# Projections with the norm's root behind the product, reordered column chunks, and head-norm products on GpSimd

## The reference

```
x32 * rsqrt(mean(x32 * x32) + eps) * gain       # norm
z = h @ w_in                                    # first block: 2208 columns
z = xn @ w_in                                   # second block: 3212 columns
```

## Time and profile before

| | |
|---|---|
| median of 3 runs | 2364.22 us (2364.0 to 2368.03) |
| profiled execution | 2368.23 us, of which the span of the trace is 2366.4 us |
| busy | PE 88%, DVE 73%, PEld 56%, ACT 35%, POOL 28% |
| granted TensorE clock, mean | 0.956 |

### The profile page before, as it was taken

How to read it: one execution, slowest core, us unless ns; L and a number is a source line. 1 busy time by engine, 2 the same in 40 slices (tenths; PEclk the granted TensorE clock), 3 DMA queues, 4 the chain that set the end, 5 groups by cost and what they waited for, 6 DMA issues and landing times. The chain is left out here.

```text
span 2366.4 us, 27745 instructions
## 1 busy us (share of the span) xinstructions
PE 2077.3 (88%) x8634; PEld 1325.0 (56%) x8634; DVE 1718.5 (73%) x4157; ACT 832.0 (35%) x2042; POOL 672.2 (28%) x625
## 2 busy tenths in 40 slices
PE   7999999999979999998777788798999997777886
PEld 6779987679979665544222333396655542233332
DVE  6757777677767477778787777574776777787875
ACT  6656655666657521111111111275311211111110
POOL 1300001200001033444444444110243444444541
PEclk9999999999989899999999999998899999999999
DMA  6245432335545369999999999754499999999996
GB/s 221 107 180 181 185 137 81 138 125 186 186 141 160 132 244 420 420 421 421 421 421 422 421 420 421 270 157 152 178 420 420 421 421 421 421 422 421 421 421 264
DMA packets 138668, 700.51 MB, mean 296 GB/s; under 512 B 14392, under 2 KB 40248, under 8 KB 66872
## 3 DMA queue, kind: packets, MB, share of 16 engines
q0 software_dynamic: 73728, 536.90, 54.7%
q1 hardware_dynamic: 64824, 162.22, 19.6%
HBM read 698.03 MB, written 1.05 MB: 295 GB/s over the span
## 5 line engine op out<-in xcount | busy, mean ns | idle before, releaser
L2045 PE MATMUL bank<-ARENA 128*128 128x512 f32 x2048 | 993.7, 632 | 207.0 <-DVE ARENA L2345 205.9
L2045 PEld LDWEIGHTS bank<-ARENA 128*128 128x128 f32 x2048 | 387.8, 199 | 792.0 <-DVE ARENA L2345 415.6
L2335 DVE CUSTOM_DVE_ANT_0 ARENA<-ARENA 128x1024 f32<-128x1024 f32 x512 | 626.1, 1223 | 258.8 <-DMA ARENA<-in_uv_rows,ARENA 251.4
L1941 POOL DMA_INDIRECT ARENA<-in_uv_rows,ARENA x512 | 573.9, 1121 | 762.5 <-PE bank L2045 644.2
L154 PE MATMUL bank<-PARTS,PARTS 128*128 128x256 f32 (+3 forms) x1424 | 460.7, 324 | 12.3 <-DVE PARTS L284 7.1
L155 PE MATMUL bank<-PARTS,PARTS 128*128 128x256 f32 (+6 forms) x1488 | 470.6, 316 | 0.0
L156 PE MATMUL bank<-PARTS,PARTS 128*128 128x256 f32 (+6 forms) x1488 | 470.0, 316 | 0.0
L2153 ACT ACTIVATE ARENA<-ARENA 128x1 f32<-128x1 f32 x512 | 103.9, 203 | 1028.3 <-DVE ARENA L2335 1027.4
L155 PEld LDWEIGHTS bank<-PARTS,PARTS 128*128 128x128 f32 (+2 forms) x1488 | 285.4, 192 | 13.6 <-issue 1.0
L156 PEld LDWEIGHTS bank<-PARTS,PARTS 128*128 128x128 f32 (+2 forms) x1488 | 285.0, 192 | 13.8
L154 PEld LDWEIGHTS bank<-PARTS,PARTS 128*128 128x128 f32 x1424 | 273.4, 192 | 33.0 <-DVE PARTS L284 7.8
(11 more groups left out here) (265 smaller groups left out, 1934.3 us busy)
## 6 DMA issues: line engine op xcount, KB each, us to landing
ARENA<-in_w_up_tiles SPq DMA_DIRECT2D x44, 1024.0 KB, 7.0
ARENA<-in_w_down SPq DMA_DIRECT2D x44, 512.0 KB, 3.3
ARENA<-in_w_out SPq DMA_DIRECT2D x32, 512.0 KB, 4.2
ARENA<-in_wq_tiles SPq DMA_DIRECT2D x16, 1024.0 KB, 11.6
ARENA<-in_w_in SPq DMA_DIRECT2D x40, 384.0 KB, 4.0
ARENA<-in_w_in SPq DMA_DIRECT2D x24, 512.0 KB, 9.0
ARENA<-in_w_in SPq DMA_DIRECT2D x40, 256.0 KB, 2.9
ARENA<-in_uv_rows,ARENA POOLq DMA_INDIRECT x512, 23.0
```

The source lines that it names most:

```text
L1941: nc.gpsimd.indirect_dma_start(out=slot[i % SLOTS], out_offset=None, in_=table[:, :], in_offset=bass.IndirectOffsetOnAxis(ap=picked[:, t, ...
L2045: last = mm(row_banks[t][n][:, :], diag[i % N_DIAG], slot[i % SLOTS][:, D + n * 512:D + (n + 1) * 512], start=(c == 0), stop=(c == NPICK - ...
L2335: v.tensor_tensor_reduce(u, u, xn[:, t, :], 1.0, 0.0, ALU.mult, ALU.add, dots[:, t, c:c + 1]).then_inc(S("dots_ready"), 1)
```

## The change

The norm's root moves behind the product in four places (both first-block layers and both second-block layers). TensorE transposes X itself; the gain is still multiplied in before the product, and each row of z is multiplied by the root when ScalarE takes it out of PSUM (`mul` in place of `copy`). For a turned chunk the root is a factor of the columns: VectorE builds two diagonal tiles, TensorE multiplies them by a matrix of ones, VectorE copies the result (rstd_cols), and VectorE takes the chunk out of PSUM by a product with it (`qk_scaled`); ScalarE's fourth tap then reads that copy. In the second block the transposes go column by column, and the squares are taken after the first eight weight units.

The first weights of the second block's first layer are loaded during the first block's last feed-forward net. The chunks are reordered, so that the third chunk is followed by the gate chunk and the output gate (2304) comes between the convolved ones. Much of the interleaved work is put behind other units. The products of the head norms go from VectorE to GpSimd. Of the zero products of the first block 18 of 32 stay.

```diff
+            def pe_by_columns(pe):
+                for k in range(KD):
+                    for t in range(NT):
+                        last = nc.tensor.transpose(bank[(k + first) % 8][:, t * P:(t + 1) * P],
+                                                   X[:, t, k * P:(k + 1) * P], ident)
+                    last.then_inc(S(tag + "_turned"), 1)
...
+        IN_COLUMNS = [(0, 384), (384, 384), (1152, 256), (2688, 268), (2304, 384), (1408, 256), (2956, 256), (1664, 256),
+                      (768, 384), (1920, 384)]
...
-                            last = nc.scalar.copy(z[:, t, n0:n0 + w], in_bank(c, t)[:, 0:w])
+                            last = nc.scalar.mul(z[:, t, n0:n0 + w], in_bank(c, t)[:, 0:w], STAT[:, 120 + t:121 + t])
...
+                    else:
+                        load_w_in_2(sp, 0, 0, PIECES)
...
-                        keep_busy(32)
+                        keep_busy(18)
...
-            in_chunks = [("rows", 0, 384, z[:, :, 0:384]), ("rows", 384, 384, z[:, :, 384:768]), ("turned", 1152, 256, 0),
-                         ("rows", 2688, 268, z[:, :, ML_IF:ML_IF + 268]), ("turned", 1408, 256, 2),
-                         ("rows", 2956, 256, z[:, :, SG_UV + 256:SG_UV + 512]), ("turned", 1664, 256, 4),
-                         ("rows", 2304, 384, og), ("rows", 768, 384, sbv), ("rows", 1920, 384, vaug[:, :, :, 0:HD])]
+            in_to = [("rows", z[:, :, 0:384]), ("rows", z[:, :, 384:768]), ("turned", 0),
+                     ("rows", z[:, :, ML_IF:ML_IF + 268]), ("rows", og), ("turned", 2),
+                     ("rows", z[:, :, SG_UV + 256:SG_UV + 512]), ("turned", 4),
+                     ("rows", sbv), ("rows", vaug[:, :, :, 0:HD])]
...
+                        act.wait_ge(S("qk_scaled"), d0 // 2 + 1)
                         for i in range(2):
                             f = d0 + i
-                            nc.scalar.copy(qkc[:, f, :], out_bank(c, i)[:, 0:T])
-                            last = nc.scalar.activation(qkm[:, f, :], out_bank(c, i)[:, 0:T], ACT.Identity,
+                            last = nc.scalar.activation(qkm[:, f, :], qkc[:, f, :], ACT.Identity,
                                                         scale=conv[:, f, 3:4], bias=conv[:, f, 4:5])
...
+                def qk_scaled(dve, c):
+                    d0 = in_chunks[c][3]
+                    dve.wait_ge(S("in2_used"), KD * (c + 1))
+                    for i in range(2):
+                        last = nc.vector.tensor_tensor(qkc[:, d0 + i, :], out_bank(c, i)[:, 0:T], rstd_cols, ALU.mult)
+                    last.then_inc(S("qk_scaled"), 1)
```

ScalarE's stream of the second block:

```diff
-                        if k == 7:
+                        if k == 7 and in_chunks[c - 1][0] == "rows":
                             act_take(act, c - 1)
+                        if k == 0 and c >= 2 and in_chunks[c - 2][0] == "turned":
+                            act_take(act, c - 2)
...
-                        if (c, k) == (7, 1):
+                        if (c, k) == (8, 1):
+                            attend.magnitudes(act, 0, 1)
+                            act.wait_ge(S("m_ready"), 1)
+                            nc.scalar.activation(row(6), row(6), ACT.Exp, scale=-1.0).then_inc(S("em_ready"), 1)
+                        if (c, k) == (8, 3):
+                            attend.logs(act, 0, 1)
+                        if (c, k) == (8, 4):
                             act.drain()
                             nc.scalar.activation(uv, z[:, :, SG_UV:SG_UV + 512], ACT.Gelu_apprx_tanh)
                             act.drain()
                             nc.scalar.activation(vsq_f, uvf, ACT.Square).then_inc(S("sgv_squares"), 1)
-                        if (c, k) == (8, 0):
-                            attend.magnitudes(act, 0, 1)
-                        if (c, k) == (8, 2):
-                            attend.logs(act, 0, 1)
...
```

VectorE's stream:

```diff
-                        if c in (4, 6, 8) and k < 3:
-                            last = tap(c - 2, k)
+                        if k == 7 and in_chunks[c - 1][0] == "turned":
+                            qk_scaled(dve, c - 1)
...
+                        if c in (4, 7, 9) and 1 <= k < 4:
+                            last = tap(c - 2, k - 1)
...
-                        if (c, k) == (4, 5):
-                            dve.wait_ge(S("sb_rstd"), 1)
-                            tt(sq12, sbqk, view(ss12, (12, NT), (1, 12), (0, HD)), ALU.mult)
-                        if (c, k) == (4, 7):
-                            dve.drain()
-                            tt(sqf, sqf, view(sbg, (0, NT), (1, 768)), ALU.mult).then_inc(S("sb_ready"), 1)
...
-                        if (c, k) == (7, 6):
+                        if (c, k) == (8, 0):
                             attend.scaled(dve, 0)
                             attend.scaled(dve, 1)
-                        if (c, k) == (8, 4):
+                        if (c, k) == (8, 5):
                             attend.softplus(dve, 0)
                             attend.softplus(dve, 1)
```

GpSimd's stream and TensorE's:

```diff
+                    pool.drain()
+                    nc.gpsimd.tensor_tensor(sq12, sbqk, view(ss12, (12, NT), (1, 12), (0, HD)), ALU.mult)
+                    pool.drain()
                     pool.wait_ge(S("mix2_params"), N_PARAMS)
+                    nc.gpsimd.tensor_tensor(sqf, sqf, view(sbg, (0, NT), (1, 768)), ALU.mult).then_inc(S("sb_ready"), 1)
                     nc.gpsimd.tensor_tensor(sgw, sgw, const("tril_t", (0, SGG), (1, P)), ALU.mult).then_inc(S("sgw_ready"), 1)
...
+                    nc.gpsimd.tensor_tensor(uvv, uvv, view(ss4, (4, NT), (1, 4), (0, HD)), ALU.mult)
+                    pool.drain()
+                    nc.gpsimd.tensor_tensor(uvf, uvf, view(svg, (0, NT), (1, SGG * HD)), ALU.mult).then_inc(S("uv_ready"), 1)
...
+                        if (c, k) == (1, 7):
+                            pe.wait_ge(S("rstd_diag"), 1)
+                            nc.tensor.matmul(bank[7][:, 0:T], const("ones"), view(rstd_diag, (1, T)),
+                                             start=True, stop=True).then_inc(S("rstd_spread"), 1)
-                        if (c, k) == (4, 6):
+                        if (c, k) == (4, 4):
                             turn_if()
-                        if (c, k) == (5, 1):
+                        if (c, k) == (5, 0):
                             turn_sb()
...
-                        if (c, k) == (8, 2):
+                        if (c, k) == (8, 1):
                             attend.suffix_sums(pe, 0)
                             attend.suffix_sums(pe, 1)
```

193 lines of the change are left out of this document (97 added, 96 removed).

## The result

The changed kernel is slower, by half a per cent. Its median is 2377.6 us (5 runs, 2375.63 to 2378.18), that of the kernel before 2368.03 (5 runs, 2364.0 to 2368.88); the measured ratio is 1.0049 with an interval of 1.0037 to 1.0061, which is 11.6 us (the two medians stand 9.6 us apart). Run again beside the experiments it gave 1.0067 (1.0047 to 1.0086). 2376 was forecast.

The account below looks back on a forecast made before the run. TensorE was taken to bound the second block's projection. Its layers' +7.6 and +8.0 with the first block's -2.1 and -1.6 gave +11.9 us, 2380.1 against the profiled execution, carried to the median as 2376; range 2357 to 2386.

Parts of the forecast that it names:

- The starts: Layers' first products come earlier: -2.1 and -1.6 us in the first block, -5.1 and -6.3 in the second.
- GpSimd: Fifth chunk, second block: GpSimd's head products hold VectorE's two-input instructions, so TensorE waits; +7.7 us in each layer.
- Rival A: Fifth chunk: VectorE is not held by GpSimd's long products; 2 x 7.7 us go, 2361; chance 0.18.
- The suffix sums: TensorE waits 8.0 us for softplus behind ScalarE's gelu, plus 1.7 for a half clock: +9.7 in each layer.
- Rival B: The suffix wait is short, as VectorE and ScalarE run ahead in chunk 7; 2357; chance 0.08.
- The scores: Second block: TensorE's wait for sb_low ahead of the scores grows by 0.5 us in each layer.
- The clock: Second block's half clocks: +1.7 us behind each long wait, -1.7 at each start, -2.9 behind layer 1's scores.
- rival C: Neither long wait, at GpSimd's products or the suffix sums, comes and all small gains hold; 2341; chance 0.08.
- D: The half clock lasts 12 us once in each layer: +8.6 us, 2385; chance 0.10.

Follow-up runs that it names:

- f9: The changed kernel run once more, unaltered; ratio to the kernel before 1.0067 (1.0047 to 1.0086).
- e1: The changed kernel with only the two head-norm products put back on VectorE; ratio to the kernel before 1.0029.
- e6: The kernel before with only the two head-norm products put on GpSimd; one run, 2381.8 us.
- e5: The changed kernel with each of GpSimd's two head-norm products cut into six instructions of 256 elements; ratio to the kernel before 1.0022.
- e4: The changed kernel with head-norm products on VectorE, and ScalarE's gelu and TensorE's suffix sums both moved behind unit (8, 5); ratio to the kernel before 1.0021.
- e7: The kernel before with the root behind the product and new starts, old chunk order, head and gate products on VectorE; ratio to the kernel before 1.0014.
- f11: e4 with 15 products of zeros on TensorE ahead of the first scores; ratio to the kernel before 1.0014.
- g12: The kernel before with zero products in TensorE's waits: 13 ahead of the second block's transposes, 11 ahead of the scores; ratio to the kernel before 1.0011.
- e8: The changed kernel with zero products in TensorE's two long waits, 16 behind unit (4, 2) and 30 behind (8, 1); ratio to the kernel before 1.0035.
- e2: The changed kernel with only ScalarE's gelu and its squares moved behind unit (8, 5); ratio to the kernel before 1.0044.

## Why the prediction was right

**The starts.** The forecast said -5.1 and -6.3 in the second block. From the engines' leaving the barrier (689.08, 1531.07) to the first product it takes 3.3 and 3.1 us, where it took 8.65 and 8.67: -5.3 and -5.6. The -6.3 took the transposes at full clock, 0.14 us each; they ran at 0.21, in a half clock, so the product is 3.1 us behind the barrier and not 2.4. In the first block -2.1 was forecast. The product starts 0.3 us earlier there (13.01 for 13.28), and the squares of the next layer 0.6 earlier (348.92 for 349.54): -0.6. The step that failed is the product's time of 12.2: the four high halves start at 10.10, not at 9.6, and the product waits for a weight's low half that VectorE makes behind four of the norm's. In the second layer -1.6 was forecast; the product comes at 351.39 for 354.54, 3.15 earlier, of which 2.5 are its own. At the barrier only 1.1 of these 3.1 us were left. In this profile a half clock near 490 us lasts 7 us where it lasted 3; it differs between the runs (7 in f9 too). The half clock behind the second block's starts was to go: it cost 1.7 us at each before, and costs 1.3 and 0.3.

**GpSimd.** +7.7 in each layer was the forecast, of it 6.0 idle. The waits were 0.57 and 4.11, 4.7 us; the forecast was too high. GpSimd's first product began at 721.89, before the chunk, as the whole stretch lay earlier; and the products took 3.0 and 3.6 us, not 3.8 twice (the prediction's other estimate was 3.4). By e1 the term is 4.9 and 3.2 us, by e6 6.0 and 6.6. The mechanism is as argued. The Trainium skill (SBUF — State Buffer, "SBUF: two separate sides") says that the port pair shared by GpSimd and a VectorE instruction with two SBUF inputs is an exclusive lock for one whole instruction, not a share of the bandwidth; e5 agrees, with low halves of 0.97 us between pieces and 3.12 beside a whole product. Rival A falls.

**The suffix sums.** 8.0 us waited, forecast; 7.27 measured, with the softplus behind the gelu as worked out; the term was 0.7 too high. Rival B falls. The Trainium skill (ScalarE: Activation LUTs, "What ACT_TABLE_LOAD costs") has a drain of 1.38 us with each load, by which the wait would have been 12; from the load at 762.54 to that at 766.09 are 3.55 us, and the load, two activations, the gate row and two high halves (1.28 + 0.94 + 0.42 + 0.91) fill them. The trace disagrees with the page again.

**The scores.** +0.5 forecast, +0.9 measured (3.36 for 2.47).

**The clock.** I charged 1.7 us behind each of the two waits and took off 1.7 behind each start and 2.9 behind the first layer's scores. The half clocks lasted 7 us at the first wait, 3 behind the scores and 7 at the suffix sums, the first and last beginning inside the wait. What they cost is 2.6, 1.7 and 1.8 us in the first layer, 2.1, 1.7 and 1.6 in the second. So the charges behind the two long waits were nearly right. The mis-sized term is the scores: 1.7 was lost behind them in both layers, where the first layer was to lose nothing and the second had none before. The sum of the charges was -1.2 in the first layer and 1.7 in the second; measured were +2.6 and +3.9, 3.8 and 2.2 more. The shorter waits made up for 2.0 and 2.2 of it.

**The sum.** From first product to end the forecast had +12.7 and +14.3, 27.0 together; measured +13.9 and +12.9, 26.8. That these agree is in part luck: the idle time was forecast too high and the clock's loss too low. Up to the second block's first product -8.8 was forecast and -6.4 measured. What was not in the forecast is F, 3.9 and 3.2 us shorter by a smaller loss of clock. f9 shows that some of it comes and goes with the execution. The two profiles are 7.4 us apart, the medians 9.6, and the ratio of 1.0049 is 11.6 us, where the forecast had 11.9; that it is met so closely says no more than the range of these three. The two long waits and their causes, which made the sign, are what the prediction had right.

**What was wrong is the counterfactual.** The forecast counted each wait at its length, and rival C, the change without both waits, at 2341, faster by 1%. e4 has neither of the long waits and stands at 1.0021, about 2370; e7 has the start alone and stands at 1.0014. The starts' 11 to 12 us are real and are used up inside the projections (6.7 and 6.5 us in e7). e1 to e4 show what became of the waits: of the 12 us of idle time that e4 takes away in each layer, 4 came back as other waits, and the half clock moved with them. The forecast priced TensorE's gaps as if ScalarE and VectorE kept up once a gap was closed; by e7 ScalarE now stands waiting for VectorE's takings, both have 2.7 to 4.4 us more in the stretch, and TensorE waits for the next low half. D (a half clock of 12 us) was not seen in a projection; the longest, in e1 and f11, is 10 us.

What stays open: how much of the 6.6 us that e7 loses in each projection comes by the takings' new order, how much by the taps' new places and how much by the work no longer done ahead, which no run separates; and why g12's shorter projections do not show in its median.

## What to carry to other kernels

Before moving a long elementwise product to GpSimd, look for VectorE instructions with two SBUF inputs beside it; if some feed the engine that sets the time, cut the product into pieces shorter than that engine's slack. A start that comes earlier is worth something only if the producers of the stretch behind it have time over: compare their work per unit with the bound engine's, not only the wait that goes, and look for a copy that has moved to another engine, so that a third now waits for it. A wait at the end of a line of work on another engine is not worth its length: close it in thought, and ask which instruction of that same line is needed next.

## What the hardware showed

Zero products of TensorE in a wait kept the clock at full speed behind it (granted clock 1.00 in e8's and g12's rows, where it was 0.5), and what can be gained so is the clock's loss alone: 5.6 us of it in e8, 6.6 in g12, with no gain in the time that could be told. The half clocks come back at the same places to about 1 us in different kernels (in F at 6 to 20, 37 to 44 and 54 to 60 us in both layers of before and g12 and the first of e2), and in others at other places (at about 1 to 21 and 50 to 58 in both layers of e1 and e5); F's work at full clock is 43.5 to 45.1 us in all 26 stretches, its length 55.5 to 62.1.
